# Attention heads by key tile: the two query blocks' products with V side by side, ones-products on sums of two key tiles

## The reference

```python
def attend(q, k, v):
    s = jnp.einsum('bqhd,bkhd->bhqk', q, k).astype(jnp.float32) * (MLA_QK ** -0.5)
    p = jax.nn.softmax(s, axis=-1).astype(v.dtype)
    return jnp.einsum('bhqk,bkhd->bqhd', p, v)
...
    if ctx is None:
        y_a = attend(q, k, v)
    else:
        k_ctx, v_ctx = mla_keys_values(ctx[0], ctx[1], p['mla_w_ukv'], p['mla_kn_g'])
        y_a = blocked_attend(with_rope(q), jnp.concatenate([with_rope(k), k_ctx], axis=1),
                             jnp.concatenate([v, v_ctx], axis=1))
```

## Time and profile before

| | |
|---|---|
| Median of 3 runs | 3488.12 us (3485.32 to 3489.54) |
| The profiled execution | 3493.94 us, its span 3491.9 us |
| Granted TensorE clock over the span | 0.961 |
| PE / DVE / ACT / POOL busy | 3310.8 / 1886.1 / 875.2 / 354.6 us |

### The profile page before, as it was taken

How to read it: one execution, slowest core, us unless ns; L and a number is a source line. 1 busy time by engine, 2 the same in 40 slices (tenths; PEclk the granted TensorE clock), 3 DMA queues, 4 the chain that set the end, 5 groups by cost and what they waited for, 6 DMA issues and landing times. The chain is left out here.

```text
span 3491.9 us, 45052 instructions
## 1 busy us (share of the span) xinstructions
PE 3310.8 (95%) x18370; PEld 2972.9 (85%) x18370; DVE 1886.1 (54%) x3157; ACT 875.2 (25%) x1346; POOL 354.6 (10%) x294
## 2 busy tenths in 40 slices
PE   5999899999799999999989998999997999999998
PEld 4998766659699999999979986666696999999998
DVE  6884744547755656555467666455316444434443
ACT  3222444542311111111122224544413111111110
POOL 0000322222100000000010004222211000000000
PEclk7997999999899999999999888999998999999999
DMA  6210000014322222222021000000211111111111
GB/s 256 95 35 1 14 4 3 3 73 159 103 79 78 84 66 66 90 78 72 25 92 45 24 3 11 4 5 1 84 32 49 49 36 47 37 48 36 48 36 55
DMA packets 45092, 185.57 MB, mean 53 GB/s; under 512 B 5472, under 2 KB 8992, under 8 KB 43424
## 3 DMA queue, kind: packets, MB, share of 16 engines
q1 hardware_dynamic: 38048, 158.58, 13.1%
q0 software_dynamic: 6912, 25.17, 2.4%
HBM read 169.14 MB, written 14.59 MB: 53 GB/s over the span
## 5 line engine op out<-in xcount | busy, mean ns | idle before, releaser
L1133 PE MATMUL ps<-a_hi,gu_hi 128*128 128x384 f32 x2112 | 711.5, 337 | 30.8 <-DVE a_lo L1672 25.6
L1133 PE MATMUL ps<-a_lo,gu_hi 128*128 128x384 f32 x2112 | 709.7, 336 | 0.0
L1133 PE MATMUL ps<-a_hi,gu_lo 128*128 128x384 f32 x2112 | 709.4, 336 | 0.0
L695 PE MATMUL ps<-a_hi,w_halves 128*128 128x384 f32 x2016 | 419.0, 339 | 28.6 <-DVE a_lo L1672 24.7
L1133 PEld LDWEIGHTS ps<-a_hi,gu_hi 128*128 128x128 f32 x2112 | 399.4, 189 | 37.1 <-issue 18.3
L1133 PEld LDWEIGHTS ps<-a_lo,gu_hi 128*128 128x128 f32 x2112 | 399.7, 189 | 0.0
L1133 PEld LDWEIGHTS ps<-a_hi,gu_lo 128*128 128x128 f32 x2112 | 399.6, 189 | 0.0
L695 PEld LDWEIGHTS ps<-a_hi,w_halves 128*128 128x128 f32 x2016 | 355.8, 190 | 40.3 <-issue 30.5
L2126 DVE TENSOR_TENSOR at<-ps,sg 128x384 f32<-128x384 f32 x132 | 73.3, 556 | 545.3 <-ACT sg L1553 545.3
L1162 PE MATMUL ps<-g_hi,d_hi 128*128 128x384 f32 x1056 | 353.7, 335 | 4.3 <-DVE g_lo L2128 4.3
L1162 PE MATMUL ps<-g_hi,d_lo 128*128 128x384 f32 x1056 | 353.5, 335 | 0.0
(11 more groups left out here) (269 smaller groups left out, 4659.8 us busy)
## 6 DMA issues: line engine op xcount, KB each, us to landing
f_raw<-wgu SPq DMA_DIRECT2D x88, 512.0 KB, 4.4
diag<-wada_c POOLq DMA_DIRECT2D x48, 512.0 KB, 3.8
f_raw<-wdn SPq DMA_DIRECT2D x44, 512.0 KB, 4.4
w_raw<-win SPq DMA_DIRECT2D x32, 512.0 KB, 3.6
wada_o<-wada_b SPq DMA_DIRECT2D x24, 512.0 KB, 3.6
spill<-z SPq DMA_DIRECT2D x2, 4608.0 KB
z<-spill SPq DMA_DIRECT2D x2, 4608.0 KB, 14.1
w_raw<-wout SPq DMA_DIRECT2D x16, 512.0 KB, 4.1
```

What stands on the lines that cost most here:

```text
L695: mm = MM(ps[:, 3 * (n % 2) + b, 0:BLK], w, a[:, k, b * BLK:(b + 1) * BLK], start=(k == 0 and first), stop=(k == KC - 1 and last))
L1133: mm = MM(ps[:, 2 * (v % 2) + part, 0:BLK], w, a[:, k, b * BLK:(b + 1) * BLK], start=(k == 0 and j == 0), stop=(k == KC - 1 and j == 2))
```

## The change

The order of the steps becomes key tile by key tile: for each of the nine key tiles first query block 0, then block 1; the prompt comes in as step 12. The exponentials get six buffers instead of three. Then:

- V is 64 columns wide in the product, and the two query blocks of one key tile are multiplied one behind the other into the two halves of the partitions of bank 6 (`weigh`, nine pairs a head). The prompt keeps its product of 128 columns, into bank 2 (`weigh_first`).
- DVE adds the exponentials of two key tiles (`pair_sum`, eight additions of 128x512 a head), and only the sums, and the ninth tile, are multiplied with 64 columns of ones into bank 7 (`totals`, five pairs a head).
- ACT makes the inverse of the denominators as exp(-ln d) (`inverted`), and DVE refines it with one Newton step of two instructions (`refined_inverse`), instead of `reciprocal`.
- `products` fixes the steps: V pairs in steps 3, 5, 7, 9, 11, 14, 16 and 18 and in step 1 of the next head, ones-pairs in 6, 10, 15 and in 0 and 2 of the next head, the prompt's product in 14. The evictions, `inverted`, `divided`, `yhigh` and `low` get new steps.

```diff
-        at_steps = [(qb, kt) for qb in range(2) for kt in range(1, KTILES)] + [(2, 0)]
+        def place(j, q):
+            return 2 * j + q + (2 * j >= S_PROMPT)
+        at_steps = [(qb, kt) for kt in range(1, KTILES) for qb in range(2)]
+        at_steps.insert(S_PROMPT, (2, 0))
...
-                    MM(ps[:, bank, 0:n], va[h % 2][:, kt], pt[:, g % 3, 0:n], start=first,
-                       stop=(kt == 0 or kt == KTILES - 1)).then_inc(at_pv.sem, 1)
+                def weigh(h, j):
+                    if j == 0:
                         pe.wait_ge(at_va.sem, at_va.at(l, h + 1))
+                        if h:
+                            pe.wait_ge(at_evv.sem, at_evv.at(l, h))
+                    pe.wait_ge(at_exp.sem, at_exp.at(l, STEPS * h + place(j, 1) + 1))
+                    for q in range(2):
+                        mm = MM(ps[DH * q:DH * q + DH, 6, :], values_side(h)[0][:, j + 1, :], p_of(h, j, q), start=(j == 0), stop=(j == 8))
+                    mm.then_inc(at_pv.sem, 1)
...
+                def totals(h, i):
+                    if i == 0 and h:
+                        pe.wait_ge(at_evd.sem, at_evd.at(l, h))
+                    if i < 4:
+                        pe.wait_ge(at_ps.sem, at_ps.at(l, 8 * h + 2 * i + 2))
+                    for q in range(2):
+                        mm = MM(ps[DH * q:DH * q + DH, 7, :], ones[:, 0:DH], psum2[:, q, :] if i < 4 else p_of(h, 8, q), start=(i == 0), stop=(i == 4))
+                    mm.then_inc(at_dn.sem, 1)
+
+                def products(h, st):
+                    if h and st < 3:
+                        if st == 0:
+                            totals(h - 1, 3)
+                        if st == 1:
+                            weigh(h - 1, 8)
+                        if st == 2:
+                            totals(h - 1, 4)
+                    if h == H:
+                        return
+                    for j in range(8):
+                        if st == place(j + 1, 1):
+                            weigh(h, j)
+                    if st == S_PROMPT + 2:
+                        weigh_first(h)
+                    if st in (6, 10, 15):
+                        totals(h, (6, 10, 15).index(st))
...
-                    if g >= 2:
-                        weigh(g - 2)
+                    products(h, st)
...
+                    own.link(A(yinv[:, 0:n], dens[:, q0:q0 + n], ACT.Ln))
+                    A(yinv[:, 0:n], yinv[:, 0:n], ACT.Exp, scale=-1.0).then_inc(at_lnx.sem, 1)
...
-                    ins = V.reciprocal(part, part)
+                    link(STT(part, part, -1.0, y_, ALU.mult, ALU.mult))
+                    STT(part, part, 2.0, y_, ALU.add, ALU.mult).then_inc(at_rec.sem, 1)
+
+                def pair_sum(h, i, q):
+                    dve.wait_ge(at_exp.sem, at_exp.at(l, STEPS * h + place(2 * i + 1, q) + 1))
+                    if i or h:
+                        dve.wait_ge(at_dn.sem, at_dn.at(l, 5 * h + i if i else 5 * h - 1))
+                    TT(psum2[:, q, :], p_of(h, 2 * i, q), p_of(h, 2 * i + 1, q), ALU.add).then_inc(at_ps.sem, 1)
...
+                        for i in range(4):
+                            for q in range(2):
+                                if j == 0 and st == place(2 * i + 1, q) + 1:
+                                    pair_sum(h, i, q)
```

More of the change, by code:

```diff
@@ L491, in units_at, with p_of @@
             return range(CUT_MAX[st], CUT_MAX[st + 1])
-        def o_bank(h, o):
-            return 6 + (h + o) % 2
+        def p_of(h, j, q):
+            return pt[:, (STEPS * h + place(j, q)) % 6, :]
         def values_side(h):
@@ L1110, in _ @@
                         max_rows(h + 1)
-                    if g >= 2:
-                        weigh(g - 2)
+                    products(h, st)
                     for u in units[len(units) // 2:]:
                         max_unit(h + 1, u)
-                weigh(STEPS * H - 2)
-                weigh(STEPS * H - 1)
+                for st in range(3):
+                    products(H, st)
                 for n in range(16, 24):
@@ new lines, in exponentials, with released @@
+                    A(pt[:, g % 6, 0:n], ps[:, src, 0:n], ACT.Exp, scale=SCALE_A).then_inc(at_exp.sem, 1)
+                def released(h, st):
+                    o, kt = at_steps[st]
+                    if o == 2:
+                        act.wait_ge(at_pp.sem, at_pp.at(l, h + 1))
+                    else:
+                        act.wait_ge(at_pv.sem, at_pv.at(l, 9 * h + kt))
+                        if kt < 9:
+                            act.wait_ge(at_ps.sem, at_ps.at(l, 8 * h + 2 * ((kt - 1) // 2) + o + 1))
+                        else:
+                            act.wait_ge(at_dn.sem, at_dn.at(l, 5 * h + 5))
@@ new lines, in evict_values, with evict_totals @@
+                def evict_values(h):
+                    half = slice(DH * (h % 2), DH * (h % 2) + DH)
+                    act.wait_ge(at_pv.sem, at_pv.at(l, 9 * h + 9))
+                    if h >= 2:
+                        act.wait_ge(at_done.sem, at_done.at(l, 3 * (h // 2)))
+                    for q in range(2):
+                        ins = A(tsum[half, SEQ + 512 * q:SEQ + 512 * (q + 1)], ps[DH * q:DH * q + DH, 6, :], ACT.Copy)
+                    ins.then_inc(at_evv.sem, 1)
+                def evict_totals(h):
+                    half = slice(DH * (h % 2), DH * (h % 2) + DH)
+                    act.wait_ge(at_dn.sem, at_dn.at(l, 5 * h + 5))
+                    for q in range(2):
+                        ins = A(dens[half, SEQ + 512 * q:SEQ + 512 * (q + 1)], ps[DH * q:DH * q + DH, 7, :], ACT.Copy)
+                    ins.then_inc(at_evd.sem, 1)
@@ new lines, in evict_first @@
+                def evict_first(h):
+                    e = h % 2
+                    half, other = slice(DH * e, DH * e + DH), slice(DH - DH * e, P - DH * e)
+                    act.wait_ge(at_pp.sem, at_pp.at(l, h + 1))
+                    if h >= 2:
+                        act.wait_ge(at_done.sem, at_done.at(l, 3 * (h // 2 - 1) + 1))
+                    A(tsum[half, 0:SEQ], ps[half, 2, 0:SEQ], ACT.Copy)
+                    A(dens[half, 0:SEQ], ps[other, 2, 0:SEQ], ACT.Copy).then_inc(at_evp.sem, 1)
@@ L1515, in _ @@
                             first_root(h + 2)
[L1516 to L1521 removed]
+                    if h and st == 1:
+                        evict_values(h - 1)
+                    if h and st == 2:
+                        evict_totals(h - 1)
+                    if st == S_PROMPT + 3:
+                        evict_first(h)
+                    if h % 2 and st == 16:
+                        inverted(h // 2, 2)
+                    if h and h % 2 == 0:
+                        if st in (5, 8):
+                            inverted(h // 2 - 1, (5, 8).index(st))
+                        if st in (3, 9, 13):
+                            yhigh(h // 2 - 1, {3: 2, 9: 0, 13: 1}[st])
                     if h == H - 1 and st in (6, 9):
                         w_high(16 + st // 9)
[L1524 to L1526 removed]
+                evict_values(H - 1)
+                evict_totals(H - 1)
+                for o in range(2):
+                    inverted(H // 2 - 1, o)
+                for o in (2, 0, 1):
                     yhigh(H // 2 - 1, o)
@@ L2064, in _ @@
                             partial_sums(h + 2, 9 + 5 * j, 14 + 5 * j)
-                        if h % 2 and st >= 15:
-                            inverses(h // 2, 0, 2 * (st - 15) + j, 2 * (st - 15) + j + 1)
+                        for i in range(4):
+                            for q in range(2):
+                                if j == 0 and st == place(2 * i + 1, q) + 1:
+                                    pair_sum(h, i, q)
                     if h + 1 < H:
@@ L2073, in _ @@
                         inverse(h + 2)
-                    if h and h % 2 == 0 and st == 4:
-                        inverses(h // 2 - 1, 2)
-                    if h and h % 2 == 0 and 5 <= st < 9:
-                        inverses(h // 2 - 1, 1, 2 * (st - 5), 2 * (st - 5) + 2)
-                inverses(H // 2 - 1, 2)
-                inverses(H // 2 - 1, 1)
+                    if h % 2 and st == 17:
+                        refined_inverse(h // 2, 2)
+                    if h and h % 2 == 0 and st in (6, 9):
+                        refined_inverse(h // 2 - 1, (6, 9).index(st))
+                for o in range(2):
+                    refined_inverse(H // 2 - 1, o)
                 def f_low(slot, count, dst, hi):
```

99 lines of the change are left out of this document (46 added, 53 removed).

## The result

The changed kernel takes **3598.4 us** (median of 4 runs, 3596.4 to 3600.7) against 3488.8 for the kernel before it: 1.031 times as long, interval 1.029 to 1.033. The forecast was 3550, in a range of 3500 to 3590. The direction was right; the size was 48 us short, and the range ended 8 us too low.

A forecast was written before the change was run, and what follows sets the result against it. In heads 0 to 6 a relay between PE units and DVE reductions over bank 5 was taken to bound the loop. +4.0 us a head made 31 a layer, +62 in two, so 3550 us; range 3500 to 3590.

The forecast's parts named there:

- steps 1 to 5: Heads 1 to 6, relay between PE, ACT and DVE before proj_q: PE late, +1.1 us together.
- What bounds the loop: Heads 0 to 6, steps 5 to 16: PE units and DVE reductions alternate over bank 5, two links of 1.09 us a step.
- The price of a pair: Two 64-column matmuls alone between 128-column work: 0.86 + 0.35 = 1.21 us, against 0.87 for a whole-width product.
- The sum over steps: Heads 1 to 6, all step terms added: +4.0 us a head.
- Pairs in links: Steps 6, 7, 9, 10, 11, 15, 16, pair between two PE units: +0.27 us each, +1.9 a head.
- the doubled reduction: Step 12, partial sum and pair sum between DVE's two reductions: second starts 1.75 us after the first, +0.66.
- steps 17 and 18: End of a head: step 17 loses its product, -0.87 us; step 18 gets a pair for a product, +0.34.
- 24 + 2.8 + 1.3: One layer's loop: heads 1 to 6 cost 24 us more, head 0 2.8, head 7 1.3.
- 2.5 + 0.6: Layer's tail: pairs left after the last score, +2.5 us; output projection's eighth k-chunk late by 0.6.
- rival (e): PE's waits in steps 8, 12, 13 drop the clock to 1.2 GHz; a tenth of the loop costs 70: 3620; chance 0.04.
- (b): Rival: PE alone sets all steps, so 1.3 us a head, +20 in all, 3508; chance 0.09.
- 0.8 twice: Head 6, steps 6 and 9, new Ln, Exp and refinements without projections over them: +0.8 us each, less 0.2 four times.

The follow-up runs named there:

- experiment 6: Changed kernel with three idle matmuls in steps 12 and 13, against that kernel with some pairs moved next to each other: 3558.4 us against 3557.1.
- experiment 8: Kernel before the change, with only the reciprocals replaced by Ln and Exp on ACT and a refinement on DVE: 3489.0 us against 3489.8, ratio 0.9994.
- experiment 3: Changed kernel with three idle matmuls added in step 13 alone, not in step 12: 3594.1 us.
- experiment 4: Changed kernel with two V pairs moved, from step 11 to 12 and from 14 to 13, nothing added: 3577.8 us.
- experiment 7: Changed kernel with one DVE pair sum moved from step 12 to 14: 3592.9 us; with idle matmuls in steps 12 and 13 as well: 3569.5 us.
- the last kernel of experiment 7: Changed kernel with idle matmuls in steps 12 and 13, and one DVE pair sum moved from step 12 to the end of step 13: 3562.5 us.

## Why the prediction was right and wrong

**The loss, taken apart.** 3598.4 - 3488.8 = 109.6 us. Idle matmuls give back 41.3 of it: the clock. Whole-width matmuls in place of pairs give back 50.8 more: the change of width. What is left, 3506.4 against 3489.8 in that comparison, is 16.6. In that kernel's trace the two loops are 7.9 and 3.8 us longer than before (the doubled link of step 13, a later relay in steps 1 to 5, and some 6 us of clock), and about the rest lies in the tails.

**What bounds the loop: right.** Links without a pair stayed at 1.09 (534.98 to 536.07 above), steps 8 and 12 at 2.18; products taken out of them saved nothing.

**The price of a pair: right.** 1.21 was forecast. In head 7 a step with 0.70 of scores and a pair takes 1.90, so a pair costs 1.20. PE's timeline of the changed kernel, step 7 of head 7, with weight loads (PEld):

```profile
828.24 0.50 PE L1074 MATMUL ps<-qh,kh 97*128 97x512 f32 x1
...
828.57 0.39 PE L1075 MATMUL ps<-ql,kh 96*128 96x512 f32 x1
828.57 0.19 PEld L1076 LDWEIGHTS ps<-qh,kl 96*128 96x128 f32 x1
828.80 0.40 PE L1076 MATMUL ps<-qh,kl 96*128 96x512 f32 x1
829.12 0.20 PEld L1086 LDWEIGHTS ps<-pt,va 128*64 128x64 f32 x4 [0.36 <-issue]
829.13 1.08 PE L1086 MATMUL ps<-pt,va 128*64 128x512 f32 x4
830.13 0.19 PEld L1074 LDWEIGHTS ps<-qh,kh 97*128 97x128 f32 x1 [0.81 <-ACT pt L1509]
830.14 0.50 PE L1074 MATMUL ps<-qh,kh 97*128 97x512 f32 x1
...
830.47 0.39 PE L1075 MATMUL ps<-ql,kh 96*128 96x512 f32 x1
```

From the last score to the pair it is 0.33 where a score costs 0.23, the pair takes 1.01 where it streams for 0.86, and the first score behind it takes 0.33 again: 0.10 + 0.15 + 0.10, the 0.34 of experiment 6 but for rounding. The loads show how. Between matmuls of one width a load starts with the matmul ahead (828.57, both). At a change of width it starts 0.01 ahead of its own matmul, so it lies in the open. (The exponential named in brackets is not one that this score waits for.) In experiment 6 the second pair's load starts 0.43 ahead of its matmul (807.30 for 807.73), and that pair costs 0.86.

Of the two pages of the Trainium skill that the prediction weighed, the rule of "TensorE: Matmul & The Clock Gate", Part 3, that a group of tiles costs one matmul plus 4 ns for each further tile, fits a pair that follows a pair (0.86), and not a pair alone (1.20). A pair alone fits "TensorEngine Tiling (Array Packing)" of the Trainium skill, Key Properties, which names a drain of the engine at a change of tiling mode and gives no price for it. Here it is 50.8 us over 224 pairs, 0.23 a pair, as some stand where PE waits anyway.

**The sum over steps: nearly right, in part by errors that cancel.** With the clock held, head 1 costs 50.49 - 46.17 = 4.3 us more; 4.0 was forecast. Pairs in links came to 0.28 each (0.27), step 14 to 0.50 (0.5). Two terms were too large: steps 1 to 5 came to 0.8 instead of 1.1, and the doubled reduction to 0.53 instead of 0.66 (unit starts 1.63 apart, 536.07 to 537.70, for 1.75; it shows one step later than named, since it is the unit of step 13 that waits). One was too small: steps 17 and 18 together were to save 0.5 and cost 0.15, because step 18, which was forecast to keep its score, had held the prompt's, of 128 columns, and in the new order holds a full one. A loop cost 29.9 us more in the second layer with the clock held; the forecast's 24 + 2.8 + 1.3 is 28.1.

**The tail: right in sum only, by luck.** 2.5 + 0.6 was forecast. PE reaches the output projection 1.8 us later than before (three pairs in a row behind the first cost 0.86 each, not 1.21), and then waits 1.33 us longer for the eighth chunk. Together 3.1. The chain to POOL's last `low`, which the prediction put at 11.5 (its terms add up to 11.4), took 12.3 (848.72 to 861.03).

**The step that failed is the clock: the sum has no term for it.** The prediction put it at nothing in the forecast and left it to rival (e), that PE's waits in steps 8, 12 and 13 might "drop the granted clock to 1.2 GHz in part of the loop", with 4 chances in 100. Its one reason was a row: "Before, the loop held 0.99". That row could not speak against it, as no step before the change is as thin: among the steps of heads 0 to 6 the thinnest before is step 16, with PE busy for 2.63 us of 3.28, where step 12 now has 1.17 of 2.19. The prediction's own relay said how thin they would be: a step of 2.18 us with no product and, in step 12, the prompt's small score. The runs showed in its place a granted clock of 0.92, and 41.3 us that come back when those steps are filled. Without that loss the forecast would have stood: 3557.1 with the clock held, 7 above the 3550 and inside the range. The range made room for the pair, for DVE and for (b), and none for a loss that comes on top of the forecast.

The size in (e) was off too: 70 us were forecast for a tenth of the loop at 1.2 GHz. 0.92 over 400 us is about 60 us a loop at 1.2 GHz, more than a tenth, and 41 came back in both loops together; head 6 kept its stretch in one of them, and where a relay sets the pace a slower PE need not show.

**Reciprocals: right.** Nothing in the kernel before, as experiment 8 shows. In head 6, where the prediction expected 0.8 twice, less what the reciprocals had cost there, the refinements make steps 7 and 10 0.41 us longer than a step with a pair alone (2.89 and 2.88 for 2.48 and 2.47 in the second layer, with the clock held); what else it lost there is the pair sum of step 8.

## What to carry to other kernels

When a change takes work out of an engine that is close to being the bound, look for the steps that are left thin, and at the granted clock of the steps behind them: here filling two thin steps in each of 14 heads with useless matmuls gave back 41 us. Before halving an operation into column groups, price it as it will stand: here a pair cost 1.20 us alone between full-width work and 0.86 behind another pair. And look at what the other engine on the same memory is doing before an addition is moved to a "free" place.

## What the runs showed of the hardware

**A clock that falls without a long gap.** In the head shown, the longest wait of PE in steps 12 and 13 was 0.78 us, and the clock fell in that stretch of each of heads 0 to 5, in both layers. What PE had done just before differs from run to run: 1.17 us of work in a step of 2.19 in experiment 3, 1.54 in 2.19 in experiment 4, where nine heads of twelve lost the clock. Step 8, with 1.53 in 2.18, did not lose it in heads 0 to 5, behind steps full of projections. The Trainium skill, "TensorE: Matmul & The Clock Gate", section "A second HAM failure mode: psum-queue depth-cycling", tells of a kernel in which short idle times between groups of matmuls make the clock swing; this trace agrees, with four waits of 0.37 to 0.78 us in steps 12 and 13. What exactly decides was not settled.

**DVE and POOL hinder each other.** The same addition of two SBUF tiles took 0.68 us on DVE alone, and 1.36 and 1.83 beside POOL's multiplications; in head 7, 2.04. In the rows of experiment 7 the long sum ends 0.55 us after POOL's instruction, begun before it, has ended (535.57 + 1.63 = 537.20, and 537.75). It is the same for all 20 sums of the changed kernel that took more than 0.8 us: each began inside a POOL instruction and ended 0.55 us after its end. The other way round, POOL's next instruction in those rows takes 2.24 us, against 1.79 in the last kernel of experiment 7, where no sum is beside it. The Trainium skill, "SBUF — State Buffer", section "SBUF: two separate sides", says that a DVE instruction with two SBUF inputs and a GpSimd one that reads SBUF lock each other out for whole instructions; these rows fit it. The forecast took the sum's price from a row with an operand in PSUM and had no place for it.
